# Expert weights in one 32 KB run per partition, x2 in natural order, and a 64x64 transpose of the expert activation

## The chip, the cores and the metric

One of the cores of a Trainium2 chip runs the whole program; the other cores are idle. The metric is the device time of one execution in microseconds (us), from the first to the last instruction of the program with what lies around them. Three runs were taken of the kernel before.

## The reference

One layer of a hybrid encoder block, for 256 tokens with 1024 features, all in float32:

```
h = rmsnorm(x, g_mix);  proj = h @ w_in
y_lru = rg_lru(conv(lru_x)) * gelu(lru_gate)          # gated linear recurrence
y_fox = forgetting_attention(q, k, v, cum_logf)       # 16 heads of 64
x = x + (sigmoid(gate_lru) * (y_lru @ w_lru_out)
         + sigmoid(gate_fox) * (y_fox @ w_fox_out)) @ w_o
t = rmsnorm(x, g_ffn)
logits = t @ w_router + b_router                      # top 4 of 32, softmax over the 4
for e in range(32):
    gu = t @ w_gate_up[e] + b_gate_up[e]              # 1024 x 2048
    gate = min(gu[:, :1024], 7);  up = clip(gu[:, 1024:], -7, 7)
    y = ((up + 1) * gate * sigmoid(1.702 * gate)) @ w_down[e] + b_down[e]   # 1024 x 1024
    out = out + combine[:, e] * y
return rmsnorm(x + out, g_final)
```

## The kernel before, in words

Every instruction stream is written out by hand, with semaphores between the engines. SP issues nearly all DMAs in one fixed order, TensorE (PE) runs the products, ScalarE (ACT) and VectorE (DVE) empty the PSUM banks.

**The mixers** run first, as 40 chunks of weights of 1024 x 256. Each chunk is 1 MB, loaded in runs of 1 KB, split into a high and a low part (L491 on ACT, L735 on DVE) and multiplied at L1135. The last four chunks (C_WO) give `x2`, the residual stream, at L931: there DVE adds the product to x and writes `x2` so that the features 2n and 2n+1 of each 256 columns lie in two separate halves (`as_read`). PE transposes `x2` (L1239), multiplies it with the router weights (L1245), and DVE chooses the experts.

**The experts** follow, 32 in 16 pairs. An expert gets up to 64 slots; a table `sel` of zeros and scales picks the tokens. For each expert PE does, in this order:

- `gate_up`: two bias products (L1301), then 8 chunks of 128 rows of the weights, each with 4 products of 512 columns (L1308). The stationary operand is `hg`, 128 features x 64 slots; two products at a time use the two column halves of the array.
- `gather_half` (L1295): half of the gather for the next pair, 4 blocks of 128 features x 2 token tiles, stationary `x2`, moving `sel`.
- `transpose_selW` (L1315) once per pair, `scatter` of the expert before into the accumulators (L1339), in two parts around
- `transpose_act` (L1320), which brings the activation `up` from slots x features to features x slots, for `actT`. `up` holds two halves of 512 features, on partitions 0-63 and 64-127.
- `down`: a bias product (L1325), then 4 chunks with 4 products each (L1332).

DVE and ACT compute the activation (L1024 to L1031, L640), copy the gathered tokens with the gain g_ffn (L634 on ACT, L1018 on DVE), and copy `actT` (L644) and the output (L652). At four of the experts PE adds `x2` to the accumulators (L1289).

**The order of a sum over features.** A load puts several rows of a weight matrix on one partition, since that makes the run in memory longer. Which features share a partition decides which features must be together in `hg` or `actT`. Before, two consecutive rows of w_gate_up (8 KB each) and four of w_down (4 KB each) lie on a partition, 16 KB in one run; so `x2` is stored by two, and the transposes of the activation read by four.

**The loads of the experts** are planned by `plan()`: a chunk is 8 KB per partition, and there are 23 places for chunks. The first 24 chunks are loaded one by one (1 MB), then by pairs (2 MB, one run of 16 KB), and from the ninth expert to the thirtieth by four (4 MB); the last two experts are loaded by pairs again. A load by four consists of two runs of 16 KB on each partition, whose addresses lie 2 MB apart. SP waits for PE's count `chunk_done` until the place is free (L341, L343, L346) and issues the load; PE waits for the whole load before its first chunk.

```
src = w_gate_up[bass.ds(e, 1), c * P:(c + 4) * P, :] if c < GU_CHUNKS else w_down[bass.ds(e, 1), :, :]
sp.dma_start(quads[p][:, :].rearrange("p (m x) -> p m x", m=2),
             src.rearrange("e (m p i) n -> p (e m) (i n)", m=2, p=P)).then_inc(loaded[p], 16)
```

**The vectors** (gains and biases) are loaded by ACT at the start (L463 to L465), transposed by PE (L1098, L1099) and copied to `vec` (L727). L512 is the first to read them. A branch for more than 64 tokens per expert ends the program's expert stage; the records have one pass over the experts.

Of the kernel before, what the change touches and what calls it, by code (L numbers as in the profile page):

```python
# [14 lines left out]
P = 128  # L15
# [13 lines left out]
CC = 256  # L29
# [47 lines left out]
EARLY = {20: 0, 24: 1, 32: 2, 36: 3}  # L77
NVEC = 72
V_GMIX, V_CONVW, V_CONVB, V_BRG, V_BIG, V_LAM, V_GFFN = 0, 8, 40, 48, 56, 64, 72


def hybrid_block(nc, x, g_mix, w_in, conv_w, conv_b, w_rg, b_rg, w_ig, b_ig, lru_lambda, b_f,
# [3 lines left out]
    with ctx:  # L86
# [100 lines left out]

        def as_read(t):
            return t.rearrange("q t (i n) -> q t n i", i=2)

        assert [place_at[p] for p in FIRST] == [at[n] for n in (
# [23 lines left out]
        up = flat(x_sb)[:, 1024:1536]  # L215
        actT = gate.rearrange("p (j h s) -> p j h s", h=2, s=SLOTS)
        actT_late = alias("actT_late", [P, 512], F32, bias_at)[:, :].rearrange("p (j h s) -> p j h s", h=2, s=SLOTS)
        Y = flat(x_sb)[:, 1536:2048]
# [10 lines left out]
        sq = [flat(GL)[:, 0:CC], flat(GL)[:, CC:2 * CC]]  # L229
        g4 = alias("g4", [4, 2 * P], F32, lg_at)  # L230
        gain = vec[:, V_GFFN:V_GFFN + KT].rearrange("p (i m) -> p m i", i=2)
        nothing = stat[:, 68:69]
# [71 lines left out]
        def _(sp):  # L304
            for t in range(TT):
                sp.dma_start(x_sb[:, t, :], x[0, t * P:(t + 1) * P, :]).then_inc(x_loaded[t], 16)
            def piece_src(e, m):
                if m < GU_CHUNKS // 2:
                    return w_gate_up[bass.ds(e, 1), 2 * m * P:2 * (m + 1) * P, :].rearrange("e (p i) n -> p (e i n)", i=2)
                j = m - GU_CHUNKS // 2  # L310
                return w_down[bass.ds(e, 1), 4 * j * P:4 * (j + 1) * P, :].rearrange("e (p i) n -> p (e i n)", i=4)

            def chunk_src(e, c):
                return piece_src(e, c // 2)[:, c % 2 * CHUNK:(c % 2 + 1) * CHUNK]

# [17 lines left out]
            def load_expert(load):  # L333
                h, n, p = LOADS[load]
                e, c = ORDER[h]
                if AFTER[load] < 0:
                    free_after[place_at[p]]()
                else:
                    sp.wait_ge(chunk_done, MIX_CHUNKS + AFTER[load] + 1)
                if n == 1:  # L340
                    sp.dma_start(slot[p][:, :], chunk_src(e, c)).then_inc(loaded[p], 16)  # L341
                elif n == 2:
                    sp.dma_start(pairs[p][:, :], piece_src(e, c // 2)).then_inc(loaded[p], 16)  # L343
                else:
                    src = w_gate_up[bass.ds(e, 1), c * P:(c + 4) * P, :] if c < GU_CHUNKS else w_down[bass.ds(e, 1), :, :]
                    sp.dma_start(quads[p][:, :].rearrange("p (m x) -> p m x", m=2),  # L346
                                 src.rearrange("e (m p i) n -> p (e m) (i n)", m=2, p=P)).then_inc(loaded[p], 16)

            for c in range(MIX_CHUNKS):
                if c == 4:  # L350
                    sp.wait_ge(f_zeroed, 2)
                    for r0 in (0, F_REST):
                        sp.dma_start(wf[:, :, r0:r0 + HEADS], w_in[:, F_COL:F_COL + HEADS].rearrange("(k p) n -> p k n", p=P)).then_inc(small_loaded, 16)
                        sp.dma_start(bf[r0:r0 + HEADS, :], b_f.rearrange("(h a) -> h a", a=1)).then_inc(small_loaded, 16)
                    sp.dma_start(wr[:, :, :].rearrange("p (m i) n -> p m (i n)", i=2),
                                 w_router.rearrange("(m p i) n -> p m (i n)", p=P, i=2)).then_inc(small_loaded, 16)
                    sp.dma_start(brt[:, :], b_router.rearrange("(a n) -> a n", a=1).broadcast_to([P, N_EXP])).then_inc(small_loaded, 16)
# [26 lines left out]
            with sp.If(over > 0):  # L384
                sp.wait_ge(chunk_done, MIX_CHUNKS + ALL_CHUNKS)
                with sp.Fori(1, ROUNDS) as r:
                    with sp.Fori(0, N_EXP) as e:
                        for c in range(EXP_CHUNKS):
                            sp.wait_ge(chunk_done, r * ALL_CHUNKS + e * EXP_CHUNKS + (MIX_CHUNKS + c - EXP_CHUNKS + 1))
                            sp.dma_start(slot[spill + c][:, :], chunk_src(e, c)).then_inc(loaded[spill + c], 16)  # L390
            sp.end_ifs()
# [61 lines left out]
        def _(act):  # L453
# [7 lines left out]

            for src, r0 in ((g_mix, V_GMIX), (conv_b, V_CONVB), (b_rg, V_BRG), (b_ig, V_BIG), (lru_lambda, V_LAM)):
                act.dma_start(rows[r0:r0 + KT, :], src.rearrange("(j p) -> j p", p=P)).then_inc(rows_loaded, 16)  # L463
            act.dma_start(g4[:, :], g_ffn.rearrange("(m n) -> m n", m=4)).then_inc(rows_loaded, 16)
            act.dma_start(rows[8:40, :], conv_w.rearrange("w (j p) -> (w j) p", p=P)).then_inc(rows_loaded, 16)  # L465
# [165 lines left out]
            def hg_copy(p):  # L631
                act.wait_ge(gathered, p * 2 + 1)
                for k in range(KT // 2):
                    ins = act.activation(hg[:, k, :, :], ga[:, k * P:(k + 1) * P].rearrange("p (i s) -> p i s", i=2), ACT.Identity,  # L634
                                         scale=gain[:, k // 2, k % 2:k % 2 + 1])
                ins.then_inc(hga_ready, 1)
# [5 lines left out]
            def actT_copy(n, to=actT):  # L642
                act.wait_ge(act_transposed, n + 1)
                act.activation(to, pj[0][:, :].rearrange("p (j h s) -> p j h s", h=2, s=SLOTS), ACT.Identity).then_inc(actT_ready, 1)  # L644

# [56 lines left out]
        def _(dve):  # L702
# [102 lines left out]
            dve.wait_ge(small_loaded, 96)  # L805
            wr_rows = wr[:, :, :].rearrange("p (m i) n -> p m i n", i=2)
            v.tensor_tensor(wr_rows, wr_rows, gain.unsqueeze(3).broadcast_to([P, KT // 2, 2, N_EXP]), ALU.mult).then_inc(wr_ready, 1)
            split_lower(10)
# [118 lines left out]
            for c in range(4):  # L927
                if C_WO + c + 2 < MIX_CHUNKS:
                    split_lower(C_WO + c + 2)
                dve.wait_ge(chunk_done, C_WO + c + 1)  # L930
                v.tensor_tensor(as_read(x2[:, :, c * CC:(c + 1) * CC]), x_sb[:, :, c * CC:(c + 1) * CC].rearrange("q t (n i) -> q t n i", i=2),  # L931
                                pj[c % 2][:, :].rearrange("q (t n i) -> q t n i", t=TT, i=2), ALU.add).then_inc(dve_evac, 1)

# [82 lines left out]
            def hg_copy(p):  # L1016
                dve.wait_ge(gathered, p * 2 + 2)
                v.tensor_tensor(hg[:, KT // 2:, :, :].rearrange("p (m i) e s -> p m i (e s)", i=2),  # L1018
                                gb[:, :].rearrange("p (m i n) -> p m i n", m=2, i=2),
                                gain[:, KT // 4:, :].unsqueeze(3).broadcast_to([P, KT // 4, 2, P]), ALU.mult).then_inc(hgb_ready, 1)  # L1020

# [67 lines left out]
        def _(pe):  # L1089
# [4 lines left out]
            for _ in range(14):  # L1094
                mm(pj[1][:, 0:P], ident[:, :], ident[:, :], start=True, stop=True)
            pe.wait_ge(rows_loaded, 112)
            for i in range(2):
                nc.tensor.transpose(ga[:, NVEC + 4 * i:NVEC + 4 * i + 4], g4[:, :].rearrange("m (n i) -> m i n", i=2)[:, i, :], ident[0:4, 0:4])  # L1098
            nc.tensor.transpose(ga[:, 0:NVEC], rows[0:NVEC, :], ident[0:NVEC, 0:NVEC]).then_inc(vec_psum, 1)  # L1099
# [186 lines left out]
            def add_residual(t, h):  # L1286
                for m in range(2):
                    c0 = h * 512 + m * CC
                    mm(acc[t][h][:, m * CC:(m + 1) * CC], ident[:, :], x2[:, t, c0:c0 + CC].rearrange("q (i n) -> q n i", i=2),  # L1289
                       start=False, stop=True, skip_group_check=True)  # L1290

            def gather_half(b):
                for k in range(b * KT // 2, (b + 1) * KT // 2):
                    for t in range(TT):
                        last = mm((ga, gb)[b][:, k % 4 * P:(k % 4 + 1) * P], x2[:, t, k * P:(k + 1) * P], sel[:, t, :, :],  # L1295
                                  start=(t == 0), stop=(t == TT - 1))
# [21 lines left out]
            def transpose_act():  # L1318
                for j in range(4):
                    last = nc.tensor.transpose(pj[0][:, j * P:(j + 1) * P],  # L1320
                                               up.rearrange("p (r i) -> p i r", i=4)[:, j, :], ident[:, :])
                last.then_inc(act_transposed, 1)

            def down(i, chunk_at, actT=actT):
                mm(gb[:, :], onehot[:, i, :], bdn[:, :], start=True, stop=False)  # L1325
                for c in range(DN_CHUNKS):
                    w = chunk_at(GU_CHUNKS + c)
                    for a in range(2):
                        f = 2 * c + a
                        for q in range(2):  # L1330
                            h = SLOTS * q
                            last = mm(gb[h:h + SLOTS, :], actT[:, f % 4, f // 4, :],  # L1332
                                      w[:, a * D + q * 512:a * D + (q + 1) * 512], start=False, stop=(f == KT - 1))
# [79 lines left out]
            with pe.If(over > 0):  # L1413
                with pe.Fori(1, ROUNDS) as r:
                    with pe.Fori(0, PAIRS) as p:
# [7 lines left out]
                        for i in range(2):  # L1423
# [6 lines left out]
                            gate_up(i, chunk_at)  # L1430
                            pe.wait_ge(act_ready, n + 1)
                            if i == 0:
                                pe.wait_ge(selw_ready, pair + 1)
# [29 lines left out]
```

## Time and profile before

| | |
|---|---|
| median of 3 runs | 1206.67 us (1205.15 to 1209.22) |
| the profiled execution, its own time | 1204.34 us |
| its span | 1202.6 us |
| PE busy | 1162.9 us (97%) |
| weight loads (PEld) busy | 610.2 us (51%) |
| DVE, ACT busy | 339.5 us (28%), 259.7 us (22%) |
| mean granted TensorE clock | 0.992 |
| DMA | 449.84 MB, 374 GB/s over the span |
| chain that ended last | PE 70%, DMA 27%, DVE 2%, ACT 1% |

The profile names the engines PE (products), PEld (weight loads of PE, beside its products), DVE, ACT, POOL and SP. L1308 is line 1308 of the kernel. A fp32 product that is no transpose is recorded as two instructions. Busy time on PE holds the whole of each product while the next one runs into it; the distance between two starts, or the chain of work, tells what one costs.

### The profile page before, as it was taken

The numbers are of one execution on the slowest core, as the hardware profiler recorded it, in microseconds if no ns is written. First come the engines' busy times: TensorE is split into PE (matmuls) and PEld (weight loads), VectorE is DVE, ScalarE is ACT, GpSimd is POOL, SyncE is SP. The second block draws the span as 40 slices with busy tenths as digits, with TensorE's granted clock in tenths as the row PEclk, the third lists the DMA queues.
The fourth block names the chain that finished last, engine by engine and source line by source line (L and its number), as shares of the span: only waits on it lengthen the run. The fifth ranks groups of instructions, "written<-read, shape, count | busy, mean of one in ns | idle before, by whom it ended". The sixth has DMA issues, their size and how long they took to land.

```text
span 1202.6 us, 14707 instructions
## 1 busy us (share of the span) xinstructions
PE 1162.9 (97%) x6466; PEld 610.2 (51%) x6466; DVE 339.5 (28%) x653; ACT 259.7 (22%) x429; POOL 15.3 (1%) x27
## 2 busy tenths in 40 slices
PE   8999999999999999999999999999999999999997
PEld 8999999997334333333334333333333333333332
DVE  6587887564121110101021110101010101010101
ACT  6647666443001100100001100000000000010102
POOL 2000000101000000000000000000000000000000
PEclk9999999999999999999999999999999999999999
DMA  9955555788999999999999999999999999999995
GB/s 280 327 192 175 169 183 176 234 297 314 411 429 428 427 429 427 428 427 428 428 428 426 428 428 428 427 428 428 428 428 426 427 428 428 428 427 427 430 427 230
DMA packets 76714, 449.84 MB, mean 374 GB/s; under 512 B 8092, under 2 KB 49128, under 8 KB 50408
## 3 DMA queue, kind: packets, MB, share of 16 engines
q1 hardware_dynamic: 76512, 448.82, 91.7%
q8 instruction: 53, 0.87, 0.3%
q14 instruction: 13, 0.11, 0.0%
q10 hardware_dynamic: 136, 0.04, 0.0%
HBM read 447.80 MB, written 1.05 MB: 373 GB/s over the span
## 4 chain that ended last, share of the span: by engine, by line
PE 70%; DMA 27%; DVE 2%; ACT 1%; issue 0%; DVEq 0%; SPq 0%; ACTq 0%
PE pj L1308 23%; DMA quad<-in_w_gate_up 23%; PE pj L1135 17%; PE gb L1332 14%; DMA pair<-in_w_down 3%; PE gb L1295 2%; PE s L1339 2%; PE pt L1339 2%; PE ga L1295 2%; PE pj L1320 1%; PE gb L1325 1%; PE pj L1301 1%; DMA mix<-in_w_in 1%; DVE w_lo L735 1%; PE s L1198 1%; ACT w_hi L491 1%
## 5 line engine op out<-in xcount | busy, mean ns | idle before, releaser
L1308 PE MATMUL pj<-quad,GL 128*64 128x512 f32 x1408 | 316.9, 606 | 22.8 <-DMA quad<-in_w_gate_up 22.8
L1024 DVE TENSOR_SCALAR x_sb<-pj 128x512 f32<-128x512 f32 x32 | 22.1, 692 | 719.0 <-PE pj L1308 719.0
L1308 PEld LDWEIGHTS pj<-quad,GL 128*64 128x64 f32 x1408 | 99.7, 139 | 228.8 <-issue 192.1
L1332 PE MATMUL gb<-quad,x_sb 128*64 128x512 f32 x704 | 155.9, 596 | 0.0
L640 ACT ACTIVATE x_sb<-x_sb 128x512 f32<-128x512 f32 x32 | 20.1, 630 | 508.6 <-DVE x_sb L1024 508.6
L1135 PE MATMUL pj<-hT_hi,w_hi 128*128 128x256 f32 x424 | 122.0, 288 | 0.0
L1135 PE MATMUL pj<-hT_hi,w_lo 128*128 128x256 f32 x424 | 119.9, 283 | 0.0
L1135 PE MATMUL pj<-hT_lo,w_hi 128*128 128x256 f32 x424 | 118.3, 279 | 0.0
L1308 PE MATMUL pj<-pair,GL 128*64 128x512 f32 x512 | 111.6, 594 | 0.0
L735 DVE TENSOR_TENSOR w_lo<-mix,w_hi 128x1024 fp32r<-128x1024 f32 x80 | 96.2, 1244 | 41.9 <-ACT w_hi L491 41.4
L1332 PEld LDWEIGHTS gb<-quad,x_sb 128*64 128x64 f32 x704 | 48.7, 137 | 93.3 <-issue 93.3
L491 ACT ACTIVATE w_hi<-mix 128x2048 fp32r<-128x2048 f32 x40 | 76.6, 1916 | 77.5 <-PE pj L1135 72.2
L1135 PEld LDWEIGHTS pj<-hT_hi,w_hi 128*128 128x128 f32 x424 | 79.9, 188 | 2.2 <-issue 2.0
L1135 PEld LDWEIGHTS pj<-hT_lo,w_hi 128*128 128x128 f32 x424 | 80.5, 190 | 0.2
L1135 PEld LDWEIGHTS pj<-hT_hi,w_lo 128*128 128x128 f32 x424 | 79.6, 188 | 0.0
L1308 PEld LDWEIGHTS pj<-pair,GL 128*64 128x64 f32 x512 | 36.1, 137 | 71.4 <-issue 71.4
L652 ACT ACTIVATE x_sb<-gb 128x512 f32<-128x512 f32 x31 | 18.5, 597 | 230.8 <-PE gb L1332 230.8
L1332 PE MATMUL gb<-pair,x_sb 128*64 128x512 f32 x208 | 46.2, 596 | 0.0
L1339 PE MATMUL s<-x_sb,GL 64*128 64x512 f32 x128 | 36.1, 642 | 0.7 <-ACT x_sb L652 0.7
L1295 PEld LDWEIGHTS ga<-GL,x 128*128 128x128 f32 x256 | 29.8, 192 | 12.4 <-issue 12.2
L1295 PEld LDWEIGHTS gb<-GL,x 128*128 128x128 f32 x256 | 29.8, 192 | 12.2 <-issue 12.2
L1339 PE MATMUL pt<-x_sb,GL 64*128 64x512 f32 x128 | 35.9, 638 | 0.0
(300 smaller groups left out, 1108.9 us busy)
## 6 DMA issues: line engine op xcount, KB each, us to landing
quad<-in_w_gate_up SPq DMA_DIRECT2D x44, 4096.0 KB, 38.9
quad<-in_w_down SPq DMA_DIRECT2D x22, 4096.0 KB, 40.3
pair<-in_w_gate_up SPq DMA_DIRECT2D x32, 2048.0 KB, 17.7
pair<-in_w_down SPq DMA_DIRECT2D x15, 2048.0 KB, 16.7
mix<-in_w_in SPq DMA_DIRECT2D x28, 1024.0 KB, 7.1
slot<-in_w_gate_up SPq DMA_DIRECT2D x16, 1024.0 KB, 7.7
slot<-in_w_down SPq DMA_DIRECT2D x10, 1024.0 KB, 7.0
mix<-in_w_lru_out SPq DMA_DIRECT2D x4, 1024.0 KB, 5.6
```

The costliest lines, as they stand in the source:

```text
L491: act.activation(w_hi[c % 2][:, :, :], mix[c % MIX_RING].rearrange("p (k n) -> p k n", k=KT), ACT.Identity).then_inc(hi_ready, 1)
L640: act.activation(sig, gate, ACT.Sigmoid, scale=ALPHA).then_inc(sig_ready, 1)
L652: act.activation(Y, gb[:, :], ACT.Identity).then_inc(y_ready, 1)
L735: v.tensor_tensor(w_lo[c % 2][:, half, :], src[:, half, :], w_hi[c % 2][:, half, :].bitcast(F32), ALU.subtract).then_inc(ready, 1)
L1024: v.tensor_scalar(gate, pj[0][:, :], LIMIT, None, ALU.min).then_inc(gate_ready, 1)
L1135: last = mm(to, lhs, rhs, start=(k == 0 and n == 0), stop=(k == KT - 1 and n == 2))
L1198: last = mm(ps[h][:, c0:c0 + n], Q[r0:r0 + HD, j, q * P:(q + 1) * P], K[r0:r0 + HD, j, 0:n], start=False, stop=(q == 1))
L1295: last = mm((ga, gb)[b][:, k % 4 * P:(k % 4 + 1) * P], x2[:, t, k * P:(k + 1) * P], sel[:, t, :, :], start=(t == 0), stop=(t == TT - 1))
L1301: mm(pj[b][:, :], onehot[:, i, :], bgu[:, b * 512:(b + 1) * 512], start=True, stop=False)
L1308: last = mm(pj[q // 2][h:h + SLOTS, :], hg[:, c, i, :], w[:, q * 512:(q + 1) * 512], start=False, stop=(c == GU_CHUNKS - 1))
L1332: last = mm(gb[h:h + SLOTS, :], actT[:, f % 4, f // 4, :], w[:, a * D + q * 512:a * D + (q + 1) * 512], start=False, stop=(f == KT - 1))
L1339: last = mm(acc[t][q][:, :], selWT[h:h + SLOTS, i, t * P:(t + 1) * P], Y[h:h + SLOTS, :], start=first, stop=True, skip_group_check=True)
```

## The change

A load by four now takes one run of 32 KB per partition: four consecutive rows of w_gate_up, or all eight rows of w_down that lie on a partition. Loads by pairs and single loads take the matching part of the same layout, with runs of 16 KB and 8 KB as before. So features are shared out by four within each half of 512 for gate_up, and by eight for down:

- `x2` is stored in natural order; the gather reads it with a stride of four elements (`rows_of_k`), and the residual is added with one product of 512 columns instead of two of 256.
- `transpose_act` consists of 16 products with a 64x64 identity, each on one half of the rows and the same half of the columns, the activation read with a stride of eight.
- `actT` is addressed by one index; the gain comes in two layouts: g_ffn in order among `rows` for the router, and by four (`g2`, four transposes of two rows) for the gathered tokens. This is one DMA more on ACT.
- The router's weights are loaded in natural order, in runs of 128 bytes instead of 256.
- A product that fills time is added in the branch for over 64 tokens.

```
-NVEC = 72
+NVEC = 80
...
-        actT = gate.rearrange("p (j h s) -> p j h s", h=2, s=SLOTS)
+        actT = gate.rearrange("p (j s) -> p j s", s=SLOTS)
...
-        g4 = alias("g4", [4, 2 * P], F32, lg_at)
-        gain = vec[:, V_GFFN:V_GFFN + KT].rearrange("p (i m) -> p m i", i=2)
+        g2 = alias("g2", [2, 4 * P], F32, lg_at)
+        gain = vec[:, NVEC:NVEC + KT].rearrange("p (i m) -> p m i", i=4)
...
+            def load_src(e, c, n):
+                if c < GU_CHUNKS:
+                    rows, i0 = w_gate_up[bass.ds(e, 1), c // 4 * 4 * P:(c // 4 + 1) * 4 * P, :], c % 4
+                else:
+                    rows, i0 = w_down[bass.ds(e, 1), :, :], c - GU_CHUNKS
+                return rows.rearrange("e (p x) n -> p (e x n)", p=P)[:, i0 * CHUNK:(i0 + n) * CHUNK]
...
-                    src = w_gate_up[bass.ds(e, 1), c * P:(c + 4) * P, :] if c < GU_CHUNKS else w_down[bass.ds(e, 1), :, :]
-                    sp.dma_start(quads[p][:, :].rearrange("p (m x) -> p m x", m=2),
-                                 src.rearrange("e (m p i) n -> p (e m) (i n)", m=2, p=P)).then_inc(loaded[p], 16)
+                to = {1: slot, 2: pairs, 4: quads}[n][p]
+                sp.dma_start(to[:, :], load_src(e, c, n)).then_inc(loaded[p], 16)
...
+                            (g_ffn, V_GFFN)):
                 act.dma_start(rows[r0:r0 + KT, :], src.rearrange("(j p) -> j p", p=P)).then_inc(rows_loaded, 16)
-            act.dma_start(g4[:, :], g_ffn.rearrange("(m n) -> m n", m=4)).then_inc(rows_loaded, 16)
+            act.dma_start(g2[:, :], g_ffn.rearrange("(m n) -> m n", m=2)).then_inc(rows_loaded, 16)
...
-                v.tensor_tensor(as_read(x2[:, :, c * CC:(c + 1) * CC]), x_sb[:, :, c * CC:(c + 1) * CC].rearrange("q t (n i) -> q t n i", i=2),
-                                pj[c % 2][:, :].rearrange("q (t n i) -> q t n i", t=TT, i=2), ALU.add).then_inc(dve_evac, 1)
+                v.tensor_tensor(x2[:, :, c * CC:(c + 1) * CC], x_sb[:, :, c * CC:(c + 1) * CC],
+                                pj[c % 2][:, :].rearrange("q (t n) -> q t n", t=TT), ALU.add).then_inc(dve_evac, 1)
...
-                for m in range(2):
-                    c0 = h * 512 + m * CC
-                    mm(acc[t][h][:, m * CC:(m + 1) * CC], ident[:, :], x2[:, t, c0:c0 + CC].rearrange("q (i n) -> q n i", i=2),
-                       start=False, stop=True, skip_group_check=True)
+                mm(acc[t][h][:, :], ident[:, :], x2[:, t, h * 512:(h + 1) * 512], start=False, stop=True, skip_group_check=True)
...
-                        last = mm((ga, gb)[b][:, k % 4 * P:(k % 4 + 1) * P], x2[:, t, k * P:(k + 1) * P], sel[:, t, :, :],
+                        rows_of_k = x2[:, t, b * 512:(b + 1) * 512].rearrange("q (n i) -> q i n", i=4)[:, k % 4, :]
+                        last = mm((ga, gb)[b][:, k % 4 * P:(k % 4 + 1) * P], rows_of_k, sel[:, t, :, :],
...
-                for j in range(4):
-                    last = nc.tensor.transpose(pj[0][:, j * P:(j + 1) * P],
-                                               up.rearrange("p (r i) -> p i r", i=4)[:, j, :], ident[:, :])
+                for j in range(KT):
+                    for h in (0, SLOTS):
+                        last = mm(pj[0][h:h + SLOTS, j * SLOTS:(j + 1) * SLOTS], up.rearrange("p (r i) -> p i r", i=KT)[h:h + SLOTS, j, :],
+                                  ident[h:h + SLOTS, h:h + SLOTS], start=True, stop=True)
...
-                            last = mm(gb[h:h + SLOTS, :], actT[:, f % 4, f // 4, :],
+                            last = mm(gb[h:h + SLOTS, :], actT[:, f, :],
```

How the instructions move. First PE between the gate_up and the down product of an expert, before (x_sb in the fourth row is the activation `up`; s and pt are the accumulators):

```order
L1295 MATMUL ga<-GL,x_82 128x128 x8
L1315 MATMUL pj<-ident,selW 128x128 x4
L1339 MATMUL s<-x_sb,GL 128x512 x2
L1320 MATMUL pj<-ident,x_sb 128x128 x4
L1339 MATMUL pt<-x_sb,GL 128x512 x2
L1325 MATMUL gb<-bdn,onehot 128x512
L1332 MATMUL gb<-pair_110,x_sb 64x512 x8
```

and with the change:

```order
L1281 MATMUL ga<-GL,x_82 128x128 x8
L1301 MATMUL pj<-ident,selW 128x128 x4
L1326 MATMUL s<-x_sb,GL 128x512 x2
L1307 MATMUL pj<-ident,x_sb 64x64 x16
L1326 MATMUL pt<-x_sb,GL 128x512 x2
L1312 MATMUL gb<-bdn,onehot 128x512
L1319 MATMUL gb<-pair_110,x_sb 64x512 x8
```

The place and the neighbours stay, the transposes become 16 products of 64x64, and the gather has its eight products as before. Second SP, where its loads go over from pairs to four, before:

```order
L343 DMA pair_107<-in_w_down 128x4096
L343 DMA pair_108<-in_w_down 128x4096
L346 DMA quad_117<-in_w_gate_up 128x2x4096
L346 DMA quad_118<-in_w_gate_up 128x2x4096
L346 DMA quad_119<-in_w_down 128x2x4096
```

and with the change:

```order
L336 DMA pair_107<-in_w_down 128x4096
L336 DMA pair_108<-in_w_down 128x4096
L336 DMA quad_117<-in_w_gate_up 128x8192
L336 DMA quad_118<-in_w_gate_up 128x8192
L336 DMA quad_119<-in_w_down 128x8192
```

The loads keep their order, their places and their waits; only the shape of those by four differs.

## Rows read from the trace of the kernel before

**Rows 1.** The page's slices: what the DMA engines moved in each 30 us.
```profile
GB/s 280 327 192 175 169 183 176 234 297 314 411 429 428 427 429 427 428 427 428 428 428 426 428 428 428 427 428 428 428 428 426 427 428 428 428 427 427 430 427 230
```

**Rows 2.** Windows: length, busy us (instructions) of each engine, PEclk, DMA share, GB/s.
```profile
500.00:600.00 100.00, 99.99 (x476) 37.68 (x474) 12.55 (x28) 8.38 (x17) 0.00 (x0) 1.00 1.01 428
...
700.00:800.00 100.00, 92.51 (x429) 34.15 (x427) 13.89 (x32) 8.13 (x18) 0.00 (x0) 0.98 1.01 428
```

**Rows 3.** Chain of work, 600 to 700 us: start us, us, what.
```profile
616.09 0.67 PE pj L1301 x2
...
630.64 1.98 PE ga L1295 x16
...
643.31 0.66 PE pj L1301 x2
...
670.16 0.66 PE pj L1301 x2
...
697.41 38.15 DMA quad<-in_w_gate_up
```

**Rows 4.** Chain of work, 697 to 1202 us, three of its pieces.
```profile
1139.83 39.25 DMA pair<-in_w_down
...
1182.78 0.68 PE pj L1320 x4
...
1185.89 7.04 PE gb L1332 x32
```

**Rows 5.** The page's DMA issues: count, KB each, us to landing.
```profile
quad<-in_w_gate_up SPq DMA_DIRECT2D x44, 4096.0 KB, 38.9
quad<-in_w_down SPq DMA_DIRECT2D x22, 4096.0 KB, 40.3
```

**Rows 6.** The DMA view, windows 11:16, 284:291, 330:400 and 500:600 us.
```profile
DMA packets 1726, 1.74 MB, mean 348 GB/s; under 512 B 27, under 2 KB 1726, under 8 KB 1726
...
DMA packets 410, 2.97 MB, mean 424 GB/s; under 512 B 48, under 2 KB 48, under 8 KB 48
...
DMA packets 2065, 29.98 MB, mean 428 GB/s; under 512 B 235, under 2 KB 235, under 8 KB 235
...
DMA packets 2770, 42.76 MB, mean 428 GB/s; under 512 B 160, under 2 KB 160, under 8 KB 160
```

**Rows 7.** Weight loads by line: ns min/median/max, first and last start.
```profile
L1320 PEld LDWEIGHTS pj<-ident,x_sb x128: 195/210/221, 310.0 to 1183.1; 128*128 128x128 f32 x128
...
L1315 PEld LDWEIGHTS pj<-ident,selW x64: 139/141/143, 308.4 to 1156.1; 128*128 128x128 f32 x64
...
L1295 PEld LDWEIGHTS ga<-GL,x x256: 186/192/193, 288.4 to 1101.4; 128*128 128x128 f32 x128
...
L1284 PEld LDWEIGHTS pt<-ident,stat x1: 86/86/86, 308.3 to 308.3; 128*1 128x1 f32 x1
```

**Rows 8.** Timeline of PE and PEld at L1224, L1339 and L1245: start, us.
```profile
119.17 0.64 PEld L1224 LDWEIGHTS pt<-PT,V 128*64 128x64 f32 x12 [0.17 <-issue]
...
605.70 0.30 PEld L1339 LDWEIGHTS s<-x_sb,GL 64*128 64x128 f32 x4
...
282.89 0.63 PE L1245 MATMUL ga<-wr,x_sb 128*128 128x32 f32 x4
283.36 0.61 PE L1245 MATMUL gb<-wr,x_sb 128*128 128x32 f32 x4
283.81 2.03 PE L1273 MATMUL pj<-ident 128*128 128x128 f32 x16
```

**Rows 9.** DVE's writing of x2 and a contiguous operation of its size.
```profile
L931 DVE TENSOR_TENSOR x<-x_sb,pj x4: 1067/1073/1083, 265.2 to 280.3; 128x512 f32<-128x512 f32 x4
...
L1018 DVE TENSOR_TENSOR GL<-gb,vec x16: 682/684/691, 292.3 to 1130.4; 128x512 f32<-128x512 f32 x16
```

**Rows 10.** Timeline of the start: the vectors' transposes and their first reader.
```profile
8.47 0.39 PE L1098 MATMUL ga<-ident,g 4*128 4x4 f32 x2 [1.40 <-DMA rows<-in_conv_w]
...
11.20 0.46 ACT L512 ACTIVATE hT_hi<-s,vec 128x256 fp32r<-128x256 f32 x1
```

More of the change, by code:

```diff
@@ L186, in hybrid_block @@
         x2 = alias("x2", [P, TT, D], F32, hh_at)
-        def as_read(t):
-            return t.rearrange("q t (i n) -> q t n i", i=2)
         assert [place_at[p] for p in FIRST] == [at[n] for n in (
@@ L215, in hybrid_block @@
         up = flat(x_sb)[:, 1024:1536]
-        actT = gate.rearrange("p (j h s) -> p j h s", h=2, s=SLOTS)
-        actT_late = alias("actT_late", [P, 512], F32, bias_at)[:, :].rearrange("p (j h s) -> p j h s", h=2, s=SLOTS)
+        actT = gate.rearrange("p (j s) -> p j s", s=SLOTS)
+        actT_late = alias("actT_late", [P, 512], F32, bias_at)[:, :].rearrange("p (j s) -> p j s", s=SLOTS)
         Y = flat(x_sb)[:, 1536:2048]
@@ L306, in _ @@
                 sp.dma_start(x_sb[:, t, :], x[0, t * P:(t + 1) * P, :]).then_inc(x_loaded[t], 16)
[L307 to L314, printed above, removed]
+            def load_src(e, c, n):
[4 more added lines that the diff above has]
+                return rows.rearrange("e (p x) n -> p (e x n)", p=P)[:, i0 * CHUNK:(i0 + n) * CHUNK]
             def mix_split(c):
@@ L339, in load_expert @@
                     sp.wait_ge(chunk_done, MIX_CHUNKS + AFTER[load] + 1)
[L340 to L344, printed above, removed]
-                    src = w_gate_up[bass.ds(e, 1), c * P:(c + 4) * P, :] if c < GU_CHUNKS else w_down[bass.ds(e, 1), :, :]
-                    sp.dma_start(quads[p][:, :].rearrange("p (m x) -> p m x", m=2),
-                                 src.rearrange("e (m p i) n -> p (e m) (i n)", m=2, p=P)).then_inc(loaded[p], 16)
+                to = {1: slot, 2: pairs, 4: quads}[n][p]
+                sp.dma_start(to[:, :], load_src(e, c, n)).then_inc(loaded[p], 16)
             for c in range(MIX_CHUNKS):
@@ L354, in _ @@
                         sp.dma_start(bf[r0:r0 + HEADS, :], b_f.rearrange("(h a) -> h a", a=1)).then_inc(small_loaded, 16)
-                    sp.dma_start(wr[:, :, :].rearrange("p (m i) n -> p m (i n)", i=2),
-                                 w_router.rearrange("(m p i) n -> p m (i n)", p=P, i=2)).then_inc(small_loaded, 16)
+                    sp.dma_start(wr[:, :, :], w_router.rearrange("(k p) n -> p k n", p=P)).then_inc(small_loaded, 16)
                     sp.dma_start(brt[:, :], b_router.rearrange("(a n) -> a n", a=1).broadcast_to([P, N_EXP])).then_inc(small_loaded, 16)
@@ L389, in _ @@
                             sp.wait_ge(chunk_done, r * ALL_CHUNKS + e * EXP_CHUNKS + (MIX_CHUNKS + c - EXP_CHUNKS + 1))
-                            sp.dma_start(slot[spill + c][:, :], chunk_src(e, c)).then_inc(loaded[spill + c], 16)
+                            sp.dma_start(slot[spill + c][:, :], load_src(e, c, 1)).then_inc(loaded[spill + c], 16)
             sp.end_ifs()
@@ L459, in link @@
                 act.wait_ge(act_step, steps[0])
-            for src, r0 in ((g_mix, V_GMIX), (conv_b, V_CONVB), (b_rg, V_BRG), (b_ig, V_BIG), (lru_lambda, V_LAM)):
+            for src, r0 in ((g_mix, V_GMIX), (conv_b, V_CONVB), (b_rg, V_BRG), (b_ig, V_BIG), (lru_lambda, V_LAM),
+                            (g_ffn, V_GFFN)):
                 act.dma_start(rows[r0:r0 + KT, :], src.rearrange("(j p) -> j p", p=P)).then_inc(rows_loaded, 16)
-            act.dma_start(g4[:, :], g_ffn.rearrange("(m n) -> m n", m=4)).then_inc(rows_loaded, 16)
+            act.dma_start(g2[:, :], g_ffn.rearrange("(m n) -> m n", m=2)).then_inc(rows_loaded, 16)
             act.dma_start(rows[8:40, :], conv_w.rearrange("w (j p) -> (w j) p", p=P)).then_inc(rows_loaded, 16)
@@ L634, in hg_copy @@
                     ins = act.activation(hg[:, k, :, :], ga[:, k * P:(k + 1) * P].rearrange("p (i s) -> p i s", i=2), ACT.Identity,
-                                         scale=gain[:, k // 2, k % 2:k % 2 + 1])
+                                         scale=gain[:, 0, k:k + 1])
                 ins.then_inc(hga_ready, 1)
@@ L643, in actT_copy @@
                 act.wait_ge(act_transposed, n + 1)
-                act.activation(to, pj[0][:, :].rearrange("p (j h s) -> p j h s", h=2, s=SLOTS), ACT.Identity).then_inc(actT_ready, 1)
+                act.activation(to, pj[0][:, :].rearrange("p (j s) -> p j s", s=SLOTS), ACT.Identity).then_inc(actT_ready, 1)
             def selWT_copy(p):
@@ L805, in _ @@
             dve.wait_ge(small_loaded, 96)
-            wr_rows = wr[:, :, :].rearrange("p (m i) n -> p m i n", i=2)
-            v.tensor_tensor(wr_rows, wr_rows, gain.unsqueeze(3).broadcast_to([P, KT // 2, 2, N_EXP]), ALU.mult).then_inc(wr_ready, 1)
+            v.tensor_tensor(wr[:, :, :], wr[:, :, :], vec[:, V_GFFN:V_GFFN + KT].unsqueeze(2).broadcast_to([P, KT, N_EXP]), ALU.mult).then_inc(wr_ready, 1)
             split_lower(10)
@@ L1017, in hg_copy @@
                 dve.wait_ge(gathered, p * 2 + 2)
-                v.tensor_tensor(hg[:, KT // 2:, :, :].rearrange("p (m i) e s -> p m i (e s)", i=2),
-                                gb[:, :].rearrange("p (m i n) -> p m i n", m=2, i=2),
-                                gain[:, KT // 4:, :].unsqueeze(3).broadcast_to([P, KT // 4, 2, P]), ALU.mult).then_inc(hgb_ready, 1)
+                v.tensor_tensor(hg[:, KT // 2:, :, :].rearrange("p i e s -> p i (e s)"),
+                                gb[:, :].rearrange("p (i n) -> p i n", i=4),
+                                gain[:, 1, :].unsqueeze(2).broadcast_to([P, KT // 2, P]), ALU.mult).then_inc(hgb_ready, 1)
             def glu_of(n, chunks=None):
@@ L1095, in _ @@
                 mm(pj[1][:, 0:P], ident[:, :], ident[:, :], start=True, stop=True)
-            pe.wait_ge(rows_loaded, 112)
-            for i in range(2):
-                nc.tensor.transpose(ga[:, NVEC + 4 * i:NVEC + 4 * i + 4], g4[:, :].rearrange("m (n i) -> m i n", i=2)[:, i, :], ident[0:4, 0:4])
+            pe.wait_ge(rows_loaded, 128)
+            for i in range(4):
+                nc.tensor.transpose(ga[:, NVEC + 2 * i:NVEC + 2 * i + 2], g2[:, :].rearrange("m (n i) -> m i n", i=4)[:, i, :], ident[0:2, 0:2])
             nc.tensor.transpose(ga[:, 0:NVEC], rows[0:NVEC, :], ident[0:NVEC, 0:NVEC]).then_inc(vec_psum, 1)
@@ L1431, in _ @@
                             pe.wait_ge(act_ready, n + 1)
+                            stay_awake(1)
                             if i == 0:
```

## The prediction, made before the change was run

> **What bounds the kernel now.** I read four things, in this order. First the page's GB/s line [rows 1]: from the twelfth of the forty slices to the last but one it stands at 426 to 430. That is the expert stage, in which 402.7 MB of expert weights come in (32 experts, 12 MB = 12.58 million bytes each). Then the windows [rows 2]: TensorE is 99.99 us busy per 100 at 500:600, but 92.51 at 700:800. So the stage has two halves. The chain of waits says why. In the first half nothing but PE is on it, and an expert costs PE 643.31 - 616.09 = 27.22 us or 670.16 - 643.31 = 26.85 us [rows 3], 27.04 us in the mean. The same 12.58 MB take the DMA 12.58/0.428 = 29.4 us. PE lives on what was loaded during the mixers, gains 2.4 us per expert, and at 697.41 us it has caught up: from there the chain goes through the DMA, and the last expert load lands at 1179.1 us [rows 4]. So **the DMA rate sets the end, and PE is close behind it**.
>
> How close decides this case. The down product that ends at 697.41 is the fifteenth, the one that ends at 1192.9 [rows 4] the thirty-second. Between them lie 495.5 us for 17 experts; at 27.04 us PE would need 459.7. The slack is 35.8 us, or 1.12 us over each of 32 experts. All that the change adds to PE per expert is free up to there, and costs 32 times itself beyond.
>
> **The loads.** The 66 loads of 4 MB [rows 5] had two runs of 16 KB per partition and get one of 32 KB. Per load, each of 16 DMA engines moves 8 packets where it moved 16: 66 x 8 = 528 packets fewer per engine. What is a packet worth? The same queue, full, moves 1 KB packets at 348 GB/s, 8 KB packets at 424 and 16 KB packets at 428 [rows 6]. Per engine that is 47.1, 309 and 612.5 ns. A line through the first and the last has 37.7 ns per KB and 9.4 ns per packet, and the middle one lies near it (9.4 + 8 x 37.7 = 311). At 32 KB it gives 1216 ns against 1225 for two of 16 KB: 431 GB/s. Sum: 528 x 9.4 ns = **-5.0 us**. Bounds: no gain at all, if a run is cut again or the rate is at its own limit (loads of 2 MB at 330:400 and of 4 MB at 500:600, both in 16 KB packets, run at the same 428 [rows 6]), and 528 x (2 x 309 - 612.5) = 5.5 ns, 2.9 us, if doubling helps as it did from 8 to 16 KB. Above: a line through 1 and 8 KB alone has 37.4 ns per KB and 9.7 ns per packet, so 1207 ns at 32 KB and 528 x 18 ns = 9.6 us. I take 4.7, near the line through all three.
>
> The Trainium skill (DMA: Bandwidth & Descriptors, Why small descriptors are slow) gives the overhead between the two halves of a DMA engine as about 3 cycles per packet, which at the fabric clock it states would be some 3.5 ns, an estimate; 528 of those save 1.9 us, and the sum would end within the measurement.
>
> **The activation's transposes.** Four 128x128 transposes per expert become 16 products with a 64x64 identity. They are no transposes to the engine but fp32 products, and each fp32 product is two instructions in the trace (L1295: 8 written, x16 recorded), so 4 instructions become 32. The four take 0.68 us of the chain [rows 4]. The nearest row for narrow loads is L1224: 128x64 loads in pairs on the two column halves, 12 in 0.64 us, the last 0.137 long, one per 46 ns; there 128 columns stream, here 64 [rows 8]. That loads on different row halves overlap shows at L1339: four 128-column loads of 64 rows in 0.30 us, each 185 ns [rows 8]. L1245 shows what weight loads alone allow, since only 32 columns stream: 8 instructions in 0.47 + 0.45 us, 115 ns for 128 columns [rows 8], so some 60 ns for 64. The new stationary operand is read with a stride of 8 elements; a strided load takes 210 ns (L1320) where a contiguous one takes 192 (L1295) [rows 7], so I take 70 ns per pair: 16 x 70 = 1.1 us, **+0.45 us per expert**. Bounds: +0.2 (16 x 55 ns) and +3.0 (32 in a row at 115).
>
> **The gather.** Its stationary x2 is now read with a stride of 4 elements: 16 instructions per expert, 1.98 us [rows 3], 124 ns each. Contiguous loads of this kind take 192 ns; a transpose's load takes 141 contiguous (L1315) and 210 strided (L1320) [rows 7]. Either there is a floor near 210 that a strided load meets, and the gather goes from 192 to 210, hidden or +0.1 us; or the stride adds 69 ns to every load, +1.1 us. I take the floor: one column costs (192 - 86)/128 = 0.83 ns in the contiguous load and (210 - 86)/128 = 0.97 in the strided one, 86 being the load of a single column [rows 7]. **+0.1 us per expert**. Together PE has 0.55 us more, half of the slack: it catches up with the DMA some seven experts later, and nothing of it reaches the end.
>
> The Trainium skill (SBUF — State Buffer, SBUF "cachelines" under Door 1) says that fp32 may be strided by up to 4 elements for free. The row speaks against it at that stride, 210 ns against 141; but the rule would leave the gather at +0 and put a price on the 64x64 loads alone.
>
> **Small edits.** x2 is written in order: its last addition, on the way to the router, goes from 1.07 us to the 0.68 of a contiguous one (L1018) [rows 9]: -0.4. The small loads at the start get one more issue on ACT and two more small transposes; PE waits for them until 8.47 us, but the vector they make is first read by ACT's L512, at 11.20 us [rows 10]: +0.1. The residual's four instructions at L1289 become two longer ones, four times in all, within PE's slack: 0. The router weights' 128-byte runs lie beside the mixers: 0. At 306 to 319 us the queue runs low while no buffer comes free; half a microsecond more of PE work there costs +0.3. After the last load one set of transposes is on the path: L1320 at 1182.78 [rows 4], +0.45.
>
> **Sum.** -4.7 - 0.4 + 0.1 + 0.3 + 0.45 = -4.3 us. The profiled execution took 1204.34 us around its span of 1202.6, so 1200.1; it lies 2.3 us under the median of the three runs, 1206.67, and I forecast that median: **1202.3 us**.
>
> **Rivals.**
> *PE becomes the bound (slower).* If the stride adds its 69 ns to each of the gather's 16 loads and something like half of it to each pair of narrow ones, PE gets 1.1 + 1.0 = 2.1 us per expert, more than 1.12. The end is then 1206.7 - 35.8 + 32 x 2.1 = 1238 us; with only the gather dear (1.55) it is 1220. The deciding point is 1.0 us, the slack less what the DMA gains. For it: 210 against 141 at L1320, and the trebled number of instructions. Against it: every plain fp32 load already pays 192. Chance 0.19.
> *The packets save nothing to speak of.* A run is cut again, or 428 is the limit: 1206.7 to 1204, less the small terms, around 1206. By the skill's figure above too. For it: 2 MB and 4 MB loads at the same 428. Against it: 8 KB at 424 and 1 KB at 348. Chance 0.17.
> *Longer runs collide in memory.* The 16 engines read addresses twice as far apart. If a rate of 428 fell by 1%, 646 us of 4 MB loads (66 x 4.19 MB) cost 6.5: 1213. No row hints at it. Chance 0.05.
> The forecast keeps 0.59.
>
> **Numbers.** This kernel's measurement can tell about 0.3%, 3.6 us. The forecast lies 4.4 under the median with 2.9 to 9.6 on its main term, so some 0.73 of it counts as faster: 0.43. Slower is the first rival less its mild end, and most of the third: 0.22. The rest, 0.35, is within. The range goes from 1197 (9.6 saved) to 1216, which takes in the second and third rival and the first up to 1.4 us per expert; some 0.17 is left out, nearly all of it above.
>
> **What would show it.** Right: about 8,450 packets fewer, 430 to 431 GB/s in the slices of the 4 MB loads; L1307 some 1.1 us per expert; L1281 at 2.0 to 2.1 us for 16, its loads at 210 ns; the first wait of PE for a quad near 900 us, not 697. Wrong: loads of 260 ns or more at L1281, or 32 narrow instructions over 2 us; then PE shows no idle time at all and the GB/s line falls under 428 in the second half. Unchanged GB/s with halved packets would refute the price of a packet.

## The result, and the profile after

The changed kernel takes 1274.05 us (median of 4 runs, 1273.73 to 1274.96), the kernel before 1205.91 in the runs beside it: a ratio of 1.0565, 95% interval 1.0553 to 1.0577. It is 68 us **slower**. The forecast of 1202.3 us was wrong in sign, and the time lies far above its range. The profiled execution has a span of 1273.2 us.

What the chain of work of the changed kernel shows between 600 and 700 us (start us, us, what), against [rows 3]:

```profile
by line: PE pj L1294 50.7%; PE gb L1319 21.1%; PE ga L1281 7.9%; PE pj L1307 6.2%; PE gb L1281 3.9%; PE s L1326 3.2%; PE pt L1326 3.2%; PE pj L1287 2.0%; PE gb L1312 1.3%; PE pj L1301 0.9%
...
627.93 0.67 PE pj L1287 x2
628.60 13.88 PE pj L1294 x64
642.48 3.93 PE gb L1281 x16
646.41 1.06 PE s L1326 x4
647.47 2.07 PE pj L1307 x32
649.54 1.06 PE pt L1326 x4
650.60 0.43 PE gb L1312
651.03 7.02 PE gb L1319 x32
658.05 0.67 PE pj L1287 x2
```

The activation's transposes of the same expert in the kernel before (643.31 to 670.16 in [rows 3]):

```profile
660.90 0.75 PE pj L1320 x4
```

An expert goes from 627.93 to 658.05: 30.12 us, where it took 26.85 before. Two pieces differ, the gather (L1281) with 3.93 for 1.98 us and the activation's products (L1307) with 2.07 for 0.75: together +3.27 us. In every second expert the transposes had taken 0.68 [rows 4], and there it is +3.34. The mean is 3.30 us, three times the slack of 1.12 us per expert. The products of the weights (13.88 and 7.02 us) are what they were. In the windows (length, busy us and instructions of PE, PEld, DVE, ACT, POOL, clock, DMA share, GB/s), PE now has no idle time in either half, and the DMA has, against [rows 2]:

```profile
500.00:600.00 100.00, 100.00 (x513) 44.29 (x511) 14.08 (x32) 8.73 (x19) 0.00 (x0) 1.00 0.92 384
700.00:800.00 100.00, 100.00 (x521) 47.28 (x519) 16.75 (x36) 8.77 (x19) 0.00 (x0) 1.00 0.99 419
1000.00:1100.00 100.00, 100.00 (x512) 44.33 (x509) 14.08 (x32) 8.14 (x18) 0.00 (x0) 1.00 0.98 411
```

The page's DMA issues, against [rows 5], say whose fault the lower rate is: a load lands 15 us after its issue instead of 39, so the queue is short because places come free late, not because loads are slow.

```profile
quad<-in_w_gate_up SPq DMA_DIRECT2D x44, 4096.0 KB, 14.8
quad<-in_w_down SPq DMA_DIRECT2D x22, 4096.0 KB, 15.4
```

And the weight loads of the two lines (ns min/median/max), against [rows 7]:

```profile
L1281 PEld LDWEIGHTS ga<-GL,x x256: 307/329/330, 287.8 to 1164.7; 128*128 128x128 f32 x128
...
L1307 PEld LDWEIGHTS pj<-ident,x_sb x1024: 192/213/216, 314.3 to 1252.7; 64*64 64x64 f32 x171
```

The gather's loads take 329 ns instead of 192. The 64-column loads take 213, as long as a strided transpose's load of 128 columns did.

### The profile page after: what moved, and what is told of

Its sections match the earlier page's. It is cut to its first block, busy times and chain, and to the rows that moved or that the text cites. A ratio compares the mean times of both kernels' runs of the same rounds, so it can differ in the third digit from the quotient of the medians.

```text
span 1273.2 us, 16488 instructions
## 1 busy us (share of the span) xinstructions
PE 1255.5 (99%) x7356; PEld 714.6 (56%) x7356; DVE 339.6 (27%) x653; ACT 259.8 (20%) x429; POOL 15.3 (1%) x27
## 4 chain that ended last, share of the span: by engine, by line
PE 97%; DVE 1%; ACT 1%; DMA 1%; issue 0%; SPq 0%; DVEq 0%; ACTq 0%
PE pj L1294 35%; PE gb L1319 18%; PE pj L1123 17%; PE pj L1307 5%; PE ga L1281 5%; PE gb L1281 5%; PE s L1326 3%; PE pt L1326 3%; PE pj L1287 2%; PE gb L1312 1%; DMA mix<-in_w_in 1%; PE pj L1301 1%; PE s L1186 1%; PE pt L1199 0%; PE s L1181 0%; PE ga L1153 0%
## 5 line engine op out<-in xcount | busy, mean ns | idle before, releaser
L1294 PE MATMUL pj<-quad,GL 128*64 128x512 f32 x1408 | 307.0, 594 | 0.0
L1307 PEld LDWEIGHTS pj<-ident,x_sb 64*64 64x64 f32 x1024 | 64.0, 212 | 23.7 <-issue 23.0
L1307 PE MATMUL pj<-ident,x_sb 64*64 64x64 f32 x1024 | 68.4, 283 | 0.0
L1281 PEld LDWEIGHTS ga<-GL,x 128*128 128x128 f32 x256 | 60.9, 328 | 12.4 <-issue 12.2
L1281 PEld LDWEIGHTS gb<-GL,x 128*128 128x128 f32 x256 | 60.9, 328 | 12.2 <-issue 12.2
L1281 PE MATMUL ga<-GL,x 128*128 128x128 f32 x256 | 64.0, 403 | 0.0
```

The lines of the kernel that those rows point to most:

```text
L1281: last = mm((ga, gb)[b][:, k % 4 * P:(k % 4 + 1) * P], rows_of_k, sel[:, t, :, :], start=(t == 0), stop=(t == TT - 1))
L1294: last = mm(pj[q // 2][h:h + SLOTS, :], hg[:, c, i, :], w[:, q * 512:(q + 1) * 512], start=False, stop=(c == GU_CHUNKS - 1))
L1307: last = mm(pj[0][h:h + SLOTS, j * SLOTS:(j + 1) * SLOTS], up.rearrange("p (r i) -> p i r", i=KT)[h:h + SLOTS, j, :], ident[h:h + SLOTS, h ...
```

## The experiments

Two questions were open: whether the 68 us are all PE's, and what the long runs themselves are worth; then why a strided load costs this much.

### The loads alone

The kernel before with `load_src` and the one-run DMA of the changed kernel, nothing else. Its features meet the wrong weights.

```
...
-                    sp.dma_start(quads[p][:, :].rearrange("p (m x) -> p m x", m=2),
-                                 src.rearrange("e (m p i) n -> p (e m) (i n)", m=2, p=P)).then_inc(loaded[p], 16)
+                to = {1: slot, 2: pairs, 4: quads}[n][p]
+                sp.dma_start(to[:, :], load_src(e, c, n)).then_inc(loaded[p], 16)
```

> The kernel before with the new loads only: one run of 32 KB per partition in the 66 loads of 4 MB, everything on PE as before (so the features meet the wrong weights). Theory A: the extra 67 us of the change are PE work (the strided gather and the small transposes), and the loads themselves are cheaper; by the packet times of the changed kernel's trace, 1213 ns for 32 KB against 2 x 612, this is 528 x 11 ns = 6 us faster than before, near 1200 us, with 431 to 432 GB/s in the stage of 4 MB loads. Rival B: the long runs are the slow part (the changed kernel moved only 384 to 419 GB/s there); then this kernel is slower than before, at about 410 GB/s near 1240 us. Rival C: run length makes no difference, 1206 us.

Measured: 1200.29 us, ratio 0.9954 (0.9940 to 0.9968). The DMA view at 500 to 1100 us, here and then in the kernel before:

```profile
DMA packets 8886, 258.51 MB, mean 431 GB/s; under 512 B 983, under 2 KB 983, under 8 KB 983
```
```profile
DMA packets 16632, 256.53 MB, mean 428 GB/s; under 512 B 973, under 2 KB 973, under 8 KB 973
```

In the same time 0.77% more comes in: 1225 ns for two packets of 16 KB become 1216 for one of 32 KB, 9 ns per packet saved. The long runs are 5.0 us faster (3.9 to 7.2 by the interval), and rivals B and C fall.

### Each cost put back by itself

In the changed kernel, the gather reads 128 consecutive features (e1), or the activation is transposed in four 128x128 transposes as before (e2), or both (e3). In each the features are out of order.

```
-                        rows_of_k = x2[:, t, b * 512:(b + 1) * 512].rearrange("q (n i) -> q i n", i=4)[:, k % 4, :]
+                        rows_of_k = x2[:, t, k * P:(k + 1) * P]
```

> The changed kernel with the gather reading 128 consecutive features of x2 (contiguous, the wrong ones), transposes as changed. Theory A (PE is the bound, its additions simply add up): the gather goes back from 3.93 to 1.98 us per expert, PE per expert to 27.04 + 1.39 = 28.4 us, and the time to 1274 - 31 x 1.95 = 1214 us or a little above. Rival D (the gather costs what it costs because of waits around it, not because of the stride): it stays near 1274 us. Rival B (long runs slow): stays above 1240 us.

> The changed kernel with the four 128x128 transposes of before in place of the 16 products of 64x64 (order of features wrong), the gather strided. Theory A: transposes back from 2.07 to 0.68 us, PE per expert 27.04 + 1.95 = 29.0 us, time 1274 - 32 x 1.39 = 1230 us. Rival D: if the gather alone sets the time through waits, 1270 us.

> The changed kernel with both put back (gather contiguous, four 128x128 transposes): its new loads and its small edits alone. Theory A: PE 27.0 us per expert again, the DMA is the bound again: 1200 us, as the loads alone give. A difference to the loads alone would be the price of the small edits, within 1 us. Rival B: 1240 us.

Measured: e1 1214.72 us (ratio 1.0082, 1.0065 to 1.0099), e2 1229.57 (1.0202, 1.0185 to 1.0219), e3 1200.26 (0.9958, 0.9945 to 0.9971). In e1 the gather is back at 1.98 us and the products stay at 2.07; in e2 the gather stays at 3.93:

```profile
817.00 1.98 PE ga L1281 x16
...
820.48 2.07 PE pj L1307 x32
```
```profile
800.56 3.93 PE gb L1281 x16
...
805.55 0.68 PE pj L1306 x4
```

Theory A holds to 1 us in each. The small edits (start, x2, residual) are too small to see: e3 and the loads alone have the same median, and the interval of each is some 3 us wide.

### The slack, measured by filling it

The kernel before with 4 or 8 products of 128 columns more on PE ahead of the activation's transposes (below the edit with 4). Nothing is left out of the computation.

```
                 pe.wait_ge(act_ready, n + 1)
+                stay_awake(4)
                 transpose_act()
```

> The kernel before with 4 products of 128 columns (8 instructions, about 0.95 us) more on PE ahead of the activation's transposes, a pure addition without any other change. It tests the slack of 35.8 us (1.12 us per expert). By it 31 x 0.95 = 29 us fit in: the time stays at 1206 to 1207 us. If the slack were smaller (the waits in the trace count only some 23 us), 1212 us or more.

> The same with 8 products (16 instructions, about 1.9 us per expert), beyond the slack: 1206.7 - 35.8 + 32 x 1.9 = 1231 us; by the smaller slack of 23 us 1244 us.

Measured: 1207.03 us (1.0013, 1.0004 to 1.0023) and 1226.42 us (1.0173, 1.0156 to 1.0190). The first, +0.9 us per expert, is all but free; of the second, two pieces of the chain:

```profile
655.27 1.98 PE pj L1273 x16
657.25 0.48 PE pj L1320 x4
```

Since the transposes behind them cost 0.48 instead of 0.68 here, the addition is 1.8 us, and 1205.9 - 35.8 + 32 x 1.8 = 1227.7, 1.3 us above what was measured: the slack of 35.8 us stands. The smaller one, PE's visible waits of 22.8 us, would have given 1241. A count of the idle time understates what an engine can take; the distance between two of its pieces against their work gives it.

A part of the difference can be seen in the kernel before. Behind four of PE's waits for a load, 32 products of gate_up took 8.78 us where they took 7.09 behind the others, together 6.8 us. Two pieces of the chain, and the window of the first:

```profile
854.62 8.78 PE pj L1308 x32
...
942.70 7.09 PE pj L1308 x32
```
```profile
854.60:863.40 8.80, 8.78 (x33) 2.69 (x33) 0.00 (x0) 0.00 (x0) 0.00 (x0) 0.81 1.01 428
```

PE had stood still for 2.31 us before the first, and the clock granted in it was 0.81, with a stretch from 856.6 to 858.6 us at 0.50, which is 1.2 GHz. Behind another wait of 2.71 us, at 795.88, the 32 products took 7.09, so not every wait of this length is followed by it. Work that fills a wait takes the place of such slower products as well.

### Number of instructions or stride

The changed kernel with the gather contiguous, and the 16 products reading 64 consecutive columns instead of every eighth.

```
...
-  ... up.rearrange("p (r i) -> p i r", i=KT)[h:h + SLOTS, j, :],
+  ... up[h:h + SLOTS, j * SLOTS:(j + 1) * SLOTS],
...
```

> The changed kernel with the gather contiguous and the 16 products of 64x64 kept, but reading 64 consecutive columns of the activation instead of a stride of eight (wrong features). It tells the number of instructions from the stride. Theory A (a strided fp32 load is read twice at the strided rate): 32 instructions in 1.0 to 1.1 us, their loads 137 ns instead of 213; PE 27.04 + 0.4 us, under the slack, so the DMA is the bound: 1201 us. Rival E (the instructions cost their 65 ns whatever they read): 2.07 us as before and 1214 us as with the gather alone put back.

Measured: 1201.36 us (0.9968, 0.9955 to 0.9980), with 1.08 us for the 32 instructions:

```profile
803.75 1.08 PE pj L1307 x32
```
```profile
L1307 PEld LDWEIGHTS pj<-ident,x_sb x1024: 129/135/135, 309.6 to 1180.1; 64*64 64x64 f32 x171
```

Rival E falls. The number of instructions costs 0.4 us per expert and is hidden; the stride adds 1.0 us more.

### Which strides are dear

The kernel before, its gather with strides of 2, 8 and 3 elements of x2 (wrong features). The edit for 2:

```
-  ... x2[:, t, k * P:(k + 1) * P], ...
+  ... x2[:, t, k * P // 256 * 256:(k * P // 256 + 1) * 256].rearrange("q (n i) -> q i n", i=2)[:, k % 2, :], ...
```

> The kernel before, its gather reading x2 with a stride of 2 elements (8 bytes; wrong features). Theory A1 (any stride above one element is read at half speed and a fp32 product's load reads twice): loads of about 310 to 329 ns, 16 instructions in about 3.8 us, the time near 1206 - 36 + 31 x 1.9 = 1229 us. Rival F (two elements in one 16-byte line come in one access, only a line per element is dear): loads about 192 to 260 ns, gather 2.0 to 2.9 us, time 1206 us or little more.

> The same with a stride of 8 elements (32 bytes). Both theories: the same 329 ns and 3.9 us as with a stride of 4 in the changed kernel, 1229 to 1231 us. Dearer loads (over 350 ns) would say that the distance itself counts.

> The kernel before, its gather reading x2 with a stride of 3 elements (12 bytes; wrong features). Stride 1 and 2 loaded in 192 and 196 ns, stride 4 and 8 in 329 and 335. Theory A2 (each new 16-byte line costs one access, and a load of 128 elements is bound by its lines: 32, 64, 128, 128 of them at strides 1, 2, 4, 8): 96 lines at 243/128 = 1.9 ns are 182 ns, and the load takes 86 + 182 = 268 ns, the gather about 3.1 us, the time 1206 to 1208 us. Rival G (a threshold: only strides of a whole line are slow): about 196 ns, 2.1 us, 1205 us. Rival H (a stride that is no power of two is slow in itself): 329 ns or more and 1229 us.

Measured, one run each: stride 2 1204.98 us, stride 8 1232.83 us, stride 3 1207.99 us. The loads by line, in the order 2, 3, 8:

```profile
L1295 PEld LDWEIGHTS ga<-GL,x x256: 192/196/197, 287.8 to 1101.5; 128*128 128x128 f32 x128
```
```profile
L1295 PEld LDWEIGHTS ga<-GL,x x256: 251/261/264, 289.2 to 1103.6; 128*128 128x128 f32 x128
```
```profile
L1295 PEld LDWEIGHTS ga<-GL,x x256: 312/335/336, 287.9 to 1128.9; 128*128 128x128 f32 x128
```

With 192 at stride 1 [rows 7] and 329 at stride 4 (above) the row is 192, 196, 261, 329, 335. Theory A1 (any stride is slow) falls with stride 2, the threshold G and rival H with stride 3. What is left is A2: less the 86 ns of a load of one column, 261, 329 and 335 are 1.82, 1.90 and 1.95 ns for each 16-byte piece that the 128 elements touch (96, 128 and 128 of them). At stride 2, 64 pieces at 1.9 would make 208 ns if the 86 ns came on top; 196 were measured, hardly more than the 192 of the contiguous load. So the pieces set the time from 96 on, and up to 64 the contiguous load's own 0.83 ns per column does. A2 is the only one of the named theories that fits all five; what happens in a load was not seen.

### Two versions that compute the reference

The first takes the 32 KB runs for w_gate_up alone, leaves w_down and the activation's transposes as before, and stores x2 by four within each half of 512, so that the gather is contiguous. The router's transposes of a half then wait for both of its chunks.

Against the changed kernel:

```
+        def as_read(t):
+            return t.rearrange("q t (i n) -> q t n i", i=4)
...
+                if n == 4 and c >= GU_CHUNKS:
+                    sp.dma_start(to[:, :].rearrange("p (m x) -> p m x", m=2),
+                                 w_down[bass.ds(e, 1), :, :].rearrange("e (m p i) n -> p (e m) (i n)", m=2, p=P)).then_inc(loaded[p], 16)
...
```

> A version that computes the reference: the 44 loads of w_gate_up in runs of 32 KB, the 22 of w_down in two runs of 16 KB as before; x2 is stored by four within each half of 512 features, so that the gather reads it contiguously, and the activation keeps its four 128x128 transposes. x2 can only be transposed for the router when both chunks of a half are there, which puts about 1 us more between the last mixer chunk and the first expert. Theory A: PE per expert is as before (27.04 us), the DMA stays the bound and gains 44 x 8 = 352 packets x 11 ns = 4 us; with 0 to 1 us back for the router 1202 to 1203 us. Rival B (long runs slow): over 1215 us. Rival C (no difference): 1206 to 1207 us.

Measured: 1201.29 us (ratio 0.9966, 0.9954 to 0.9978). It is 4 us faster than the kernel before beside it (1205.31) and 73 faster than the changed one.

The second adds w_down in long runs: VectorE writes the activation by eight, and the 16 products read it contiguously.

```
-                v.scalar_tensor_tensor(up, up, 1.0, gate, ALU.add, ALU.mult).then_inc(act_ready, 1)
+                v.scalar_tensor_tensor(sig.rearrange("p (i r) -> p r i", i=KT), up.rearrange("p (r i) -> p r i", i=KT), 1.0,
+                                       gate.rearrange("p (r i) -> p r i", i=KT), ALU.add, ALU.mult).then_inc(act_ready, 1)
```

> A version that computes the reference with all 66 loads in runs of 32 KB: x2 stored by four within each half (contiguous gather), and VectorE writes the finished activation by eight into another buffer, so that the 16 products of 64x64 read consecutive columns. The strided write is worth 0.4 us on VectorE ahead of the products, which take 1.08 us instead of 0.68: PE 27.8 to 27.9 us per expert, inside the slack. Theory A: the DMA is the bound and gains all 528 packets per engine, 5 to 6 us: 1200 to 1201 us, perhaps 1 us under the version with only w_gate_up in long runs. If the wait for VectorE is longer than 0.8 us per expert, PE becomes the bound and the time passes 1206 us.

Measured: 1204.16 us (0.9988, 0.9979 to 0.9997), 3 us more than the first. The chain at 610 us shows what is new, the strided write on VectorE (0.70 us in the kernel before), for which PE waits in every second expert:

```profile
612.43 1.05 DVE x_sb L1031
613.48 0.04 issue
613.52 1.15 PE pj L1323 x32
```

PE per expert is 27.6 us, less than the DMA's 29.2. But it catches up with the DMA only at 844 us (at 697 before), and after 1088 us no load is on the chain any more, only PE with its waits for VectorE and ScalarE. That by itself is not the 3 us: the version with 64 consecutive columns above (e7) has no load on its chain after 1087.5 us either, and took 1201.36. What the second version has and it has not is the strided write, and the wait for two chunks that the first version has too; so the write is the likely cause. From the end of gate_up to the transposes, 3.36 us pass in every second expert (610.16 to 613.52) where the gather and the scatter of that time are 3.04 us of work. Those 0.3 us do not make 3, and the remainder was not traced; the profiled execution, the fastest of eleven, shows only half of the difference (1202.71 against 1201.16 us).

## Why the prediction was wrong

- **What bounds the kernel, and the slack.** Right. The fillings confirm 35.8 us, and with the measured 3.30 us per expert the prediction's own formula gives 1205.9 - 35.8 + 32 x 3.30 = 1275.7 us, 1.7 above what was measured.
- **The loads.** Right, where they can show: 9.4 ns per packet were read off, 9 measured, -5.0 us against the -4.7 taken. The changed kernel cannot show them since it no longer waits for the DMA. The rival in which the packets save nothing fell, and so did the one of colliding runs. The 3 cycles per packet that the Trainium skill states (DMA: Bandwidth & Descriptors, Why small descriptors are slow), 3.5 ns by the prediction's estimate, are therefore not the whole of what a packet costs here, 9 ns.
- **The gather.** This is the step that failed. "I take the floor": 192 to 210 ns per load, +0.1 us per expert. Measured are 329 ns and +1.95 us. The 210 ns of a strided transpose's load [rows 7] were read as the limit of strided reading in general. But the rows held the other reading too: contiguous, a transpose's load takes (141 - 86)/128 = 0.43 ns per column and a product's 0.83, twice that. If a product's load reads each element twice, the strided 0.97 ns becomes 1.94, and (329 - 86)/128 is 1.90. My upper bound, 69 ns more per load, added the penalty once where it comes twice: 137 ns.
- **The transposes.** 70 ns per pair was taken, 130 measured (2.07 us / 16), for the same reason: 64 columns x 1.94 = 124 ns. The contiguous form's 1.08 us shows that count and overlap had been priced rightly at 1.1. Only the stride was mis-sized.
- **The rival "PE becomes the bound".** The right mechanism, at 2.1 us per expert instead of 3.30, so at 1238 us instead of 1274. The signs that the prediction names for being wrong came: 329 ns at L1281, 2.07 us for the 32 narrow instructions, PE without idle time. The count of instructions, which it calls trebled, goes from 4 to 32 by its own working. Its chance of 0.19 was too low for what rested on one reading of two load times. A bound of +3.0 us for the transposes stood in the text, with nothing of it in the range.
- **The small edits.** x2's last addition went from 1.07 to 0.68 us as forecast; together they are too small to see.

## What to carry to other kernels

Before longer DMA runs are bought with strided operands, compare the two engines' work per iteration: here 0.8% on the DMA was worth 5 us, and PE had 1.1 us per expert to give, against 3.3 asked. When an operation is moved to another form, take its price from a row of that form, contiguous and strided; where there is none, scale the penalty by how much slower the form is already, not by adding the difference once. And move the stride to where the data is written once: storing x2 by four made the long loads of w_gate_up possible, with the 32 gathers that read it back at 1.98 us each. Where the reader has to stride, a stride of 2 elements cost next to nothing here (196 against 192 ns per load), one of 3 or more did.

## What the runs showed of the hardware

- A weight load of a fp32 product on 128 columns takes 192, 196, 261, 329 and 335 ns at strides of 1, 2, 3, 4 and 8 elements. The Trainium skill (SBUF — State Buffer, Door 1, SBUF "cachelines") says that two hits per 16-byte line are needed for the full rate, and stride 2 and stride 4 agree with that; its inference that fp32 may be strided by 4 for free does not hold: 329 against 192 ns.
- A transpose's load of 128 columns at a stride of 4 takes 210 ns (141 contiguous), a fp32 product's 329 (192 contiguous). That each element is read twice fits 0.43 and 0.83 ns per column contiguous, and 0.97 and 1.90 strided; it is inferred from the times, not shown apart.
- Packets of 32 KB run at 431 GB/s, of 16 KB at 428, of 8 KB at 424, of 1 KB at 348. A line of 37.7 ns per KB and 9.4 ns per packet passes within 2 ns of all four.
- After four of PE's waits for a load, of 2.3 to 2.7 us, the granted clock fell for a few microseconds: 0.81 in the 8.8 us from 854.6 us, with 0.50 (1.2 GHz) in the middle, and 32 products took 8.78 us instead of 7.09.
